# Two fast feed-forward blocks: five quadrant sums and splits go from VectorE to GpSimd, one quadrant is worked in place, and a spacing rule for weight splits is dropped

## The reference

```python
def swiglu(h, w_in, w_out):
    gate, up = jnp.split(h @ w_in, 2, axis=-1)
    return (jax.nn.silu(gate) * up) @ w_out
```

## Time and profile before

| what | us |
|---|---|
| median of 3 runs | 3941.22 |
| lowest, highest | 3940.22, 3945.45 |
| the profiled execution, its own time | 3940.22 |
| its span in the profile | 3938.3 |
| TensorE busy (PE), share of the span | 3730.9, 95% |
| VectorE busy (DVE) | 1944.4, 49% |
| ScalarE busy (ACT) | 1543.3, 39% |
| GpSimd busy (POOL) | 1330.9, 34% |

### The profile page before, as it was taken

One profiled execution on the slowest core, in us unless ns is written; L12 is line 12 of the kernel. 1 busy time (PEld: TensorE's weight loads), 2 busy tenths in 40 slices (PEclk: granted clock), 3 DMA queues, 4 the chain that ended last, 5 costly groups with the idle time before them and its releaser, 6 DMA issues.

```text
span 3938.3 us, 52901 instructions
## 1 busy us (share of the span) xinstructions
PE 3730.9 (95%) x21907; PEld 3152.6 (80%) x21907; DVE 1944.4 (49%) x2968; ACT 1543.3 (39%) x2460; POOL 1330.9 (34%) x837
## 2 busy tenths in 40 slices
PE   7999989999999999998999999999989989999999
PEld 5877667889987677676888889999877777788887
DVE  4455566444356666766212354445458745432123
ACT  4133445333235433424422453333355527443223
POOL 2010003334343424426232434434434424353224
PEclk9999999999999999999999999999999999999999
DMA  5221123333332121124333432222422211242333
GB/s 185 74 84 33 44 91 127 99 102 107 97 115 88 33 63 50 38 59 139 106 103 102 134 107 67 68 67 71 153 74 65 59 39 41 70 143 83 98 97 108
DMA packets 463226, 342.99 MB, mean 87 GB/s; under 512 B 18073, under 2 KB 433803, under 8 KB 462987
## 3 DMA queue, kind: packets, MB, share of 16 engines
q1 hardware_dynamic: 462304, 339.35, 28.4%
q10 hardware_dynamic: 683, 0.26, 0.0%
HBM read 334.32 MB, written 5.24 MB: 86 GB/s over the span
## 4 chain that ended last, share of the span: by engine, by line
PE 77%; DVE 9%; ACT 5%; POOL 3%; DMA 3%; issue 2%; SPq 0%; ACTq 0%; POOLq 0%; DVEq 0%
PE PS L107 76%; DVE A L124 2%; PE PS L115 2%; ACT A L118 1%; POOL RWr L124 1%; POOL TM L124 1%; DVE A L132 1%; ACT L118 1%; ACT RWH L121 1%; DMA MW<-in_w_ada 1%; DMA MW<-in_mod_w 1%; DVE RWr L124 1%; DVE SM L144 1%; DVE TM L132 1%; DVE XT L124 1%
## 5 line engine op out<-in xcount | busy, mean ns | idle before, releaser
L124 POOL TENSOR_TENSOR RWr<-RW,RWH 128x1024 fp32r<-128x1024 f32 (+2 forms) x304 | 685.1, 2256 | 1590.7 <-ACT RWH L121 1584.6
L107 PE MATMUL PS<-HTH,RWH 128*128 128x512 f32 (+2 forms) x2688 | 989.2, 368 | 26.7 <-DVE HTr L124 8.6
L107 PE MATMUL PS<-HTr,RWH 128*128 128x512 f32 (+2 forms) x2688 | 956.4, 356 | 0.0
L107 PE MATMUL PS<-Ar,RWH 128*128 128x256 f32 (+2 forms) x3584 | 906.6, 343 | 20.2 <-DVE Ar L124 7.5
L107 PE MATMUL PS<-HTH,RWr 128*128 128x512 f32 (+3 forms) x2528 | 903.0, 357 | 0.0
L107 PEld LDWEIGHTS PS<-Ar,RWH 128*128 128x128 f32 x3584 | 622.8, 191 | 114.2 <-issue 21.8
L107 PE MATMUL PS<-Ar,RWr 128*128 128x256 f32 (+2 forms) x1792 | 607.3, 339 | 0.0
L107 PEld LDWEIGHTS PS<-HTH,RWH 128*128 128x128 f32 x2688 | 511.9, 190 | 118.1 <-issue 34.9
L121 ACT ACTIVATE RWH<-RW 128x1024 fp32r<-128x1024 f32 (+2 forms) x478 | 474.1, 999 | 319.2 <-DMA RW<-in_ffn_w_out 135.1
L107 PEld LDWEIGHTS PS<-HTr,RWH 128*128 128x128 f32 x2688 | 512.5, 191 | 64.1 <-issue 6.5
L107 PEld LDWEIGHTS PS<-HTH,RWr 128*128 128x128 f32 (+1 forms) x2528 | 481.3, 190 | 64.1 <-issue 0.2
(11 more groups left out here) (211 smaller groups left out, 4782.4 us busy)
## 6 DMA issues: line engine op xcount, KB each, us to landing
RW<-in_ffn_w_in SPq DMA_DIRECT2D x176, 512.0 KB, 3.8
MW<-in_mod_w SPq DMA_DIRECT2D x83, 512.0 KB, 4.0
MW<-in_w_ada SPq DMA_DIRECT2D x72, 512.0 KB, 4.4
RW<-in_ffn_w_out SPq DMA_DIRECT2D x80, 384.0 KB, 3.5
RW<-in_ffn_w_out SPq DMA_DIRECT2D x52, 512.0 KB, 3.8
RW<-in_mix_w_in SPq DMA_DIRECT2D x41, 512.0 KB, 3.8
RW<-in_ssd_w_in SPq DMA_DIRECT2D x40, 512.0 KB, 3.9
RW<-in_ev_w_in SPq DMA_DIRECT2D x24, 512.0 KB, 3.9
```

The costliest lines, as they stand in the source:

```text
L107: return self._ins(self.real and self.real.matmul(o, l, r, start=start, stop=stop, skip_group_check=True))
L124: return self._ins(self.real and self.real.tensor_tensor(out=o, in0=i0, in1=i1, op=op))
```

## The change

The four parts of the change:

- The three sums r11, r22 and r21 go from VectorE to GpSimd (step "sums" 0), and so do the low parts of T1 and T3 (step "sums" 2). VectorE keeps r12, the four differences, and the low parts of T2 and T4.
- r12 and T3 are made in place in HTF instead of TM. So r12 can't be made ahead of the end of the last up product, and "sums" 0 and 1 stand one step later each; there is one more step. The first weight sum no longer waits for T3's low part.
- The four warm products ahead of the first down product of f0 and b1 go.
- The entry of 9 calm steps for all chunk steps of both FastFfn goes.

```diff
-        T3 = (k.HTH[:, 0:4, right], k.HTL[:, 0:4, right])
+        self.B12F, T3 = k.HTF[:, 0:4, right], (k.HTH[:, 0:4, right], k.HTL[:, 0:4, right])
...
-        self.TF[3] = k.TM[:, 0:size].rearrange("p (k t) -> p k t", k=4)
+        self.TF[3] = self.B12F
...
-        out = [(self, "gate", 0, 0), (self, "gate", 0, 1), (self, "sums", 0), (self, "up", 0, 0), (self, "sums", 1),
-               (self, "up", 0, 1)]
-        out += self.downs(0, {0: 2, 2: 3, 4: 4})
+        out = [(self, "gate", 0, 0), (self, "gate", 0, 1), (self, "up", 0, 0), (self, "sums", 0), (self, "up", 0, 1),
+               (self, "sums", 1)]
+        out += self.downs(0, {0: 2, 1: 3, 3: 4, 4: 5})
...
-            for x in ((), (), (3, 2), (1, 4), ())[a[0]]:
+            for x in {2: (1, 3), 3: (2, 4)}.get(a[0], ()):
                 s.wait_ge("v.ff", key, "t", x)
-                if x == 3:
-                    s.wait_ge("pe.lin", key, "up", 0, 1)
...
-            TF = self.TF
-            if a[0] == 0:
...
-                v.tt(TF[3], *whole(self.T[3])).then_inc("v.ff", key, "r12")
-                v.tt(TF[1], *whole(self.B11)).then_inc("v.ff", key, "r11")
-                v.tt(TF[2], *whole(self.B22)).then_inc("v.ff", key, "r22")
...
+            TF, B12 = self.TF, self.B12F
+            if a[0] == 1:
+                v.wait_ge("pe.lin", key, "up", 0, 1)
+                v.tt(B12, self.T[3][0].bitcast(F), self.T[3][1].bitcast(F), ALU.add).then_inc("v.ff", key, "r12")
+                v.wait_ge("g.ff", key, "r11")
+                v.wait_ge("v.ff", key, "r12")
+                v.tt(TF[1], B12, TF[1], ALU.subtract).then_inc("v.ff", key, "t", 1)
+            elif a[0] == 2:
+                v.wait_ge("g.ff", key, "r22")
+                v.tt(B12, TF[2], B12, ALU.subtract).then_inc("v.ff", key, "t", 3)
                 v.wait_ge("v.ff", key, "t", 3)
                 v.tt(TF[2], TF[2], TF[1], ALU.subtract).then_inc("v.ff", key, "t", 2)
-            elif a[0] == 2:
-                v.tt(TF[4], self.B21[0].bitcast(F), self.B21[1].bitcast(F), ALU.add).then_inc("v.ff", key, "r21")
-                v.wait_ge("v.ff", key, "r21")
+            elif a[0] == 3:
+                v.wait_ge("g.ff", key, "r21")
                 v.wait_ge("v.ff", key, "t", 2)
                 v.tt(TF[4], TF[4], TF[2], ALU.subtract).then_inc("v.ff", key, "t", 4)
-                self.low(v, 3)
-            elif a[0] == 3:
-                self.low(v, 2)
-            else:
-                self.low(v, 1)
-                self.low(v, 4)
+            elif a[0] > 3:
+                x = 2 * a[0] - 6
+                v.wait_ge("s.ff", key, "t", x)
+                self.split(v, self.T[x], TF[x]).then_inc("v.ff", key, "t", x, "lo")
...
     def pool(self, gp, step, *a):
         k, key = self.k, self.key
-        if step in ("wb", "wc", "wd"):
+        if step == "sums":
+            if a[0] == 0:
+                gp.wait_ge("pe.lin", key, "gate", 0, 0)
+                gp.wait_ge("pe.lin", key, "gate", 0, 1)
+                for x, b, name in ((1, self.B11, "r11"), (2, self.B22, "r22"), (4, self.B21, "r21")):
+                    gp.tt(self.TF[x], b[0].bitcast(F), b[1].bitcast(F), ALU.add).then_inc("g.ff", key, name)
+            elif a[0] == 2:
+                for x in (1, 3):
+                    gp.wait_ge("s.ff", key, "t", x)
+                    gp.wait_ge("v.ff", key, "t", 2)
+                    self.split(gp, self.T[x], self.TF[x]).then_inc("g.ff", key, "t", x, "lo")
...
-                gp.wait_ge("v.ff", key, "t", 3, "lo")
...
-        'FastFfn f0': {('down', 0, 0, None): 4},
-        'FastFfn b1': {('down', 0, 0, None): 4},
...
-        if stage is gla[0]:
-            k.w.calm.update((i, 9) for i, step in enumerate(steps) if isinstance(step[0], FastFfn) and step[1][0] in "pw")
```

More of the change, by code:

```diff
@@ L1288, in tensor @@
                 p.wait_ge("v.ff", key, g, c, "up lo")
-                p.wait_ge("v.ff", key, "t", 3, "lo")
+                p.wait_ge("g.ff", key, "t", 3, "lo")
                 self.product7(p, g, c, step, self.T[3], pv, True)
@@ L1293, in tensor @@
                 p.wait_ge("v.ff", key, g, c, "s21 lo")
-                p.wait_ge("v.ff", key, "t", 1, "lo")
+                p.wait_ge("g.ff", key, "t", 1, "lo")
                 p.wait_ge("s.ff", key, g, c, "u2")
@@ L1367, in vector @@
         elif step == "sums":
-            TF = self.TF
-            if a[0] == 0:
-                v.wait_ge("pe.lin", key, "gate", 0, 0)
-                v.wait_ge("pe.lin", key, "gate", 0, 1)
-                whole = lambda b: (b[0].bitcast(F), b[1].bitcast(F), ALU.add)
-                v.tt(TF[3], *whole(self.T[3])).then_inc("v.ff", key, "r12")
-                v.tt(TF[1], *whole(self.B11)).then_inc("v.ff", key, "r11")
-                v.tt(TF[2], *whole(self.B22)).then_inc("v.ff", key, "r22")
-                v.wait_ge("v.ff", key, "r11")
-                v.tt(TF[1], TF[3], TF[1], ALU.subtract).then_inc("v.ff", key, "t", 1)
-                v.wait_ge("v.ff", key, "r22")
-                v.tt(TF[3], TF[2], TF[3], ALU.subtract).then_inc("v.ff", key, "t", 3)
-            elif a[0] == 1:
+            TF, B12 = self.TF, self.B12F
[8 more added lines that the diff above has]
+                v.tt(B12, TF[2], B12, ALU.subtract).then_inc("v.ff", key, "t", 3)
                 v.wait_ge("v.ff", key, "t", 3)
                 v.tt(TF[2], TF[2], TF[1], ALU.subtract).then_inc("v.ff", key, "t", 2)
-            elif a[0] == 2:
-                v.tt(TF[4], self.B21[0].bitcast(F), self.B21[1].bitcast(F), ALU.add).then_inc("v.ff", key, "r21")
-                v.wait_ge("v.ff", key, "r21")
+            elif a[0] == 3:
+                v.wait_ge("g.ff", key, "r21")
                 v.wait_ge("v.ff", key, "t", 2)
                 v.tt(TF[4], TF[4], TF[2], ALU.subtract).then_inc("v.ff", key, "t", 4)
-                self.low(v, 3)
-            elif a[0] == 3:
-                self.low(v, 2)
-            else:
-                self.low(v, 1)
-                self.low(v, 4)
+            elif a[0] > 3:
+                x = 2 * a[0] - 6
+                v.wait_ge("s.ff", key, "t", x)
+                self.split(v, self.T[x], TF[x]).then_inc("v.ff", key, "t", x, "lo")
         else:
@@ L1438, in vector @@
                     self.lo(v, g, c)
-    def low(self, v, x):
-        v.wait_ge("s.ff", self.key, "t", x)
-        if x == 1:
-            v.wait_ge("v.ff", self.key, "t", 2)
-        elif x == 2:
-            v.wait_ge("v.ff", self.key, "t", 4)
-        self.split(v, self.T[x], self.TF[x]).then_inc("v.ff", self.key, "t", x, "lo")
     def split(self, e, pair, raw):
@@ L1452, in pool @@
         k, key = self.k, self.key
-        if step in ("wb", "wc", "wd"):
+        if step == "sums":
[9 more added lines that the diff above has]
+                    self.split(gp, self.T[x], self.TF[x]).then_inc("g.ff", key, "t", x, "lo")
+        elif step in ("wb", "wc", "wd"):
             g, c = a
```

## The result

| | median us | lowest, highest | runs |
|---|---|---|---|
| before | 3942.55 | 3940.22, 3945.45 | 4 |
| after | 3968.97 | 3965.42, 3972.58 | 4 |

The ratio is 1.0062 with a 95% interval of 1.0047 to 1.0077: the change costs 18.5 to 30.4 us, 24.4 by the ratio (the two medians differ by 26.4). The prediction was +23.5 (3963). Eighteen executions of after took 3957.42 to 3977.87 us.

The account below looks back on a forecast made before the run. The prediction took TensorE as the bound, nearly always busy in the long product phases, so late arrivals are paid in full. Openings 14.8 plus group ends 8.7 gave +23.5 us on 3940.22: 3963; 8 in 10 range 3947 to 3976.

Parts of the forecast that it names:

- The first effect: f0's opening: GpSimd's three sums hold up VectorE's hidden low part, so TensorE's down products start 2.4 us late.
- The second effect: f0's opening: VectorE's later chain takes turns with GpSimd's low parts and differences; p6 starts 6.6 us later, first delay included.
- b1: b1's opening: VectorE and GpSimd take turns, including a GpSimd weight split between the hidden low parts; p6 8.2 us later.
- the clock falls as well: Rival: TensorE's clock falls after the openings' gaps and reaches p1 to p4, 3.5 us twice; 3970 us, chance 0.14.
- Warm products: Ahead of the first down product: dropping them costs nothing, since TensorE still waits for the hidden low part.
- Group ends: Without calm, earlier panel splits and copies delay p6 and p5: three b1 ends 8.2 us, all ends 9.7, 8.7 kept.
- the five other ends: Group ends where VectorE has the split or it moves only on ScalarE: 0.3 us each, 1.5 together.
- Only the group ends count: Rival: GpSimd's big instructions don't block VectorE, so the openings cost 0 to 2 us; 3946 us, chance 0.13.
- Group ends hidden: Rival: panels land late enough for copies and blocks to fall into slack, leaving the openings' 14.8 us; 3955, chance 0.15.
- Relief: Rival: f0's opening gets faster with VectorE rid of five sums, if GpSimd's 128x1536 takes under 2.3 us; 3937, chance 0.06.

Follow-up runs that it names:

- e10: Changed kernel with calm steps back, GpSimd's three sums and two low parts replaced by equally long zero writes that read nothing; ratio to before 1.0019.
- e11: Changed kernel with calm steps back, only GpSimd's three sums replaced by zero writes, its two low parts still reading SBUF; ratio to before 1.0032.
- e6: Changed kernel's order with calm steps and warm products back, but all sums and low parts on VectorE, none on GpSimd; ratio to before 1.0032.
- e4: Changed kernel with only the 9 calm steps put back: openings moved, no warm products; ratio to before 1.0043.
- e2: Changed kernel with the 9 calm steps and four warm products put back, so only the openings differ from before; ratio to before 1.0054.
- e1: Kernel before with only the entry of 9 calm steps taken out (also written e1_calm); ratio to before 1.0029.
- e8: Separate small kernel running VectorE and GpSimd additions alone and side by side; 128x1536 alone took 1.76 us on VectorE and 3.42 on GpSimd.

## Why the prediction held, and where it did not

**The first effect.** It said that the down products start 2.4 us late in f0. They start 4.72 us behind the last up product instead of 2.36, with three sums and one turn of VectorE's split in GpSimd's 11.35 us, as worked out. e10 and e11, in which the sums read nothing, bring back 2.36: shown. The clock, 1.00 in the first down products before, is 0.50 there in after (672 to 676); VectorE is later still, so it costs nothing in f0.

**The second effect, f0.** +6.6 forecast; p6 stands 7.5 later, of which 1.1 came off the phases, so 6.4. The turns were those described (4.31 and 5.00). What the prediction did not see is that the order would have cost as much without GpSimd: e6 has +7.2. Both are so. In after's order the turns cost 5.0 us (e10), and with the work back on VectorE its own nine instructions behind the up products cost as much (seven without turns cost 2.4, less the 1.2 that came off the phases). Moving them to the slower engine bought nothing, because their time stayed in VectorE's chain.

**b1.** +8.2 forecast, +8.9 measured. The hidden tiles' low parts take 4.42 instead of 1.95, 2.5 us late, as forecast (2.6); but the first down product needs only the first of them and starts just 0.4 us later than before, the wait of 0.84 came at the second. The two low parts of T2 and T4 took 10.00 us. About 1.5 us of the 8.9 is the clock behind the wait of 2.75: there the rival "the clock falls as well" was right, once and at 1.5 us, where it had 3.5 twice. The forecast took a fall in the down products as hidden. In after it is, but only because of the turns: with the turns of the five gone (e10) the fall and one turn with the panel split still keep b1's opening 4.0 us over before. So the 8.9 is not made of turns alone.

**Warm products.** "Dropping the warm products costs nothing in time": not in before's order, where it costs 1.5 us in b1 by the marks, because the clock falls in the down products (f0's 0.8 has no fall of the clock in it and is near the spread of the marks). The forecast had taken such a fall as hidden by VectorE; in before's order VectorE doesn't hide it. In the order of after it does (e4 against e2), so the sum did not suffer.

**Group ends.** Forecast: three ends of b1, 8.2 us, all of it waits; measured: b1's phases +8.1. Of it 6.0 is idle time, in six more waits. The other 2.1 is busy time for the same number of products: after each stop the first rows are a little longer (2.37 for the twelve of p6 against 2.24), and the last one before it runs out alone. The first wait was 1.27 at the first group end (forecast 1.45), the second 0.96 (1.3), the same at the second end, and 0.72 and 0.77 at the third. So the waits were forecast too long by 2.2 us, and 2.1 us of busy time, which the forecast did not have, made it up: that 8.2 meets 8.1 is luck. The 1.5 us for the five other ends did not come: f0's phases got +0.2 in e1. The forecast kept 8.7 of 9.7, without a row that says which 1.0 to leave out.

**The sum.** By the marks 15.3 + 8.1 = 23.4; forecast 14.8 + 8.7 = 23.5. The terms were off by at most 1.5 us, with both signs, so that the total is better than its parts.

**The rivals.** Only the group ends count: out, e2 adds 15.2 without them. Group ends hidden: out, by e1 (+8.0 in b1's phases). Relief: out, GpSimd's 128x1536 takes 3.42 (e8), not under 2.3. The clock: in part, as above.

## What to carry to other kernels

Before an elementwise instruction goes from VectorE to GpSimd, look at what VectorE runs at that time: beside instructions with two SBUF inputs (or a float32 tensor_scalar with a single one) the two take turns, and VectorE waits up to 3.4 us of GpSimd's for the 1.75 it got rid of; beside work on PSUM they don't. A value made in place in a buffer that another engine still reads can only be made after that read: count VectorE's instructions between that release and the first product that needs them, before and after: in f0 nine instead of six cost as much (7.2) as seven with their turns (7.4). A stop of TensorE can also bring its clock down behind it, and as long as another engine is later still, that costs nothing and is easily missed: take the other engine's delay away and it shows (2.7 us in b1). And an early weight split is early for the weight but late for all that is queued behind it on its engine: in b1 the nine steps of delay were worth 8 us.

## What the runs showed of the hardware that was not expected

The same program's executions differ, and the clock with them. Over 67 executions of before, 3932.4 to 3955.6 us, the mean granted clock of TensorE lay between 0.978 and 0.985, and the two go together (correlation -0.81, about 25 us for 0.01). The profiled execution of before had 0.984, after's 0.982, e1_calm's 0.977. So e1_calm's span is 25.1 us over before's, where its marks differ by 8.7 and its ratio by 11.4; the rest stands in stretches that no kernel here changed (up to f0's last up product 669.5 us in before and 678.1 in e1_calm; between f0's phases and b1's opening 1197.4 and 1208.6). After's profile shows 17.3 where the marks and the ratio have 23 to 24. The mean clock alone does not explain that, since after's is the lower one. By the marks after is 1.5 us shorter ahead of f0's last up product, 5.6 longer between f0's phases and b1's opening, and 10.1 shorter behind b1's phases (1164.3 against 1174.4), all outside the marks; why the last one is shorter is open. For a change of half a per cent the spans of two profiles are not subtracted; marks around the changed place are.
